# Delta stage with a pair's heads on the two partition halves, x turned on the host

## The chip, the cores and the metric

One core of a Trainium2 chip. The metric is the device time of one execution in microseconds, from start to end, the median of several runs. Lower is better.

## What is computed

One layer of a streaming encoder, for 4096 new frames of one stream and 16 frames of each of 8 running streams (the "sample" rows). Cut to what matters here:

```python
xn = rms_norm(h, ln_g)                       # x * rsqrt(mean(x^2)) * ln_g
proj = xn @ w_in                             # columns: q/k/v of group A, a, b, z_a, then group B
# group A, 8 heads of 64: causal conv (4 taps) + SiLU, l2-normed q and k, decay g, beta
# per block of 64 frames, S the 64x64 state of a head:
v_new = u - w @ S                            # u, w from a triangular solve within the block
o     = q_dec @ S + qk @ v_new
S     = S * g_tot + k_tail.T @ v_new
o_a   = rms_norm(o, gdn_norm_g) * silu(z_a)
# group B, 8 heads: softmax attention over a band of 576 keys, times silu(z_b)
h = h + concat(o_a, o_b) @ w_out
h = h + sigmoid(h @ w_gate) * rms_norm(p @ w_ple, ple_norm_g)
```

## The kernel before, in words

All arithmetic is float32; the large products are made of three passes over a high and a low part (`matmul3`, lines 86 to 90). The stages run one after the other with a barrier of all engines between them: `project_a` (q/k/v of group A, the convolution, the gates), `project_b` (the other columns, and the triangular systems), `delta` (the recurrence), the sample stages, `attend`, `combine`. Every engine has its own queue, written out by hand in program order, and semaphores between the queues; SP issues all DMAs.

**Stage A** (`project_a`) works on blocks of two tiles of 128 frames, twelve groups of 128 output columns each. While block b is multiplied, the two tiles of b+1 are prepared: `load_x` (L276), `square` on ScalarE (L442), `norm` on GpSimd (rstd, L393 to L395), `scale` on ScalarE (x times rstd, in place, L446), eight 128x128 `transposes` on TensorE into PSUM (L560), `full` on VectorE (times ln_g, L662), `split_hi` on ScalarE (L453), `split_lo` on VectorE (L668). `spill` stores the turned, normed x (`xT`) for `project_b`. The transposes stand behind groups 3 and 8. TensorE waits for `lo_ok` ahead of each block. VectorE convolves each group (L682, L685) after ScalarE copies it out of PSUM (L513). The weights are split at the start, in 32 pieces through seven buffers: `hi_part` on ScalarE (L458), `lo_part` on VectorE or GpSimd in turn (L265); 16 pieces before block 0, 16 within it.

**Delta stage** (`delta`): 32 tiles of two chunks of 64 frames; n is the chunk, t the tile. A pair p holds heads 2p and 2p+1 (e = 0, 1); the state `S` has a pair's heads on partitions 0 to 63 and 64 to 127. Everything with frames on the partitions (values `vt`, residuals `r`, new values `vn`, keys `kt`, outputs `o`) has chunk 0 of the tile on partitions 0 to 63 and chunk 1 on 64 to 127, all heads side by side. `half_heads(x)` are the four heads of pairs 2x and 2x+1. For one chunk:

- TensorE: `keys_state` (L1738), `queries_state` (L1749), `solved` (L1757), `outputs` of the chunk before (L1765), `new_state` (L1774), each for x = 0 and 1, four matmuls of 64x64x64 at a time. In an even chunk `prepare` follows: four whole transposes of the next tile's keys into `psA` (L1721), four of its values into `psB` (L1723).
- VectorE: `residual` (L1829, one operation per head), after odd chunks `keys` of the next tile (L1813), `state` (L1841, one operation per two pairs), in even chunks `out_sums` of the tile before (L1847).
- ScalarE: `decayed` (L1693), `new_values` (L1673), `out_rows` of the chunk before (L1680), `out_square` in even chunks (L1686), `values` of the next tile in odd ones (L1664).
- GpSimd, once a tile: `gate` (L1631), `scaled` (the next tile's queries, L1624), `out_norm` of the tile before (L1635 to L1646).
- SP, once a tile: store of the output rows (L1578), two loads of the query row scales (L1569), `UQ` (the solved systems, L1571), the gate rows (L1574), every second tile `conv_T` (L1559). It runs six tiles ahead.

Ahead of the loop the per-frame scales are loaded as rows and turned by 32 small transposes (L1781).

Of the kernel before, what the change touches and what calls it, by code (L numbers as in the profile page):

```python
# [31 lines left out]
P = 128  # L32
# [82 lines left out]
def project_a(nc, d, s):  # L115
# [13 lines left out]
    RING, SLOTS = 6, 7  # L129
# [4 lines left out]
    with ExitStack() as stack:  # L134
# [3 lines left out]
        x_raw = [ph.sb(f"a_x{i}", [P, D]) for i in range(2)]  # L138
        squares = ph.sb("a_squares", [P, D], mybir.dt.bfloat16)
        x_full = [ph.sb(f"a_x_full{i}", [P, KT, P]) for i in range(2)]  # L140
# [30 lines left out]
        psT = ph.ps("a_psT", [P, KT * P])  # L171
# [16 lines left out]
        x_in = [ph.sem(f"a_x_in{i}") for i in range(2)]  # L188
# [3 lines left out]
        scaled = ph.sem("a_scaled")  # L192
        xT_ps = ph.sem("a_xT_ps")
# [19 lines left out]
        spilled = [ph.sem(f"a_spilled{i}") for i in range(2)]  # L213
# [48 lines left out]
        def lo_part(eng, m, done):  # L262
            k, a, b = PIECES[m]
            eng.wait_ge(w_hi_ok, m + 1)
            eng.tensor_tensor(w_lo[:, k, a:b], stage[m % SLOTS][:, 0:b - a], w_hi[:, k, a:b].bitcast(F32),  # L265
                              ALU.subtract).then_inc(done, 1)
# [4 lines left out]
        def _(sp):  # L271
            def load_x(t):
                if t >= 2:
                    sp.wait_ge(xT_ps, t - 1)
                src = d.x_p[order[t] * P:(order[t] + 1) * P, :] if t != SAMPLE else d.x_s
                sp.dma_start(x_raw[t % 2][:, :], src).then_inc(x_in[t % 2], 16)  # L276

            def spill(t):
                sp.wait_ge(full_ok, t + 1)
                sp.dma_start(d.xT[order[t]], x_full[t % 2][:, :, :]).then_inc(spilled[t % 2], 16)  # L280
# [36 lines left out]
            load_x(0)  # L317
            with nc.allow_non_contiguous_dma(reason="small per-channel constants, once"):
                sp.dma_start(lnT[:, :], d.ln_g.rearrange("(k p) -> p k", p=P)).then_inc(ln_in, 16)
            load_x(1)  # L320
            for m, (k, a, b) in enumerate(PIECES):
# [5 lines left out]
                if m == 5:  # L327
                    with nc.allow_non_contiguous_dma(reason="small per-channel constants, once"):
# [4 lines left out]
                        sp.dma_start(alog[0:HA, :], d.a_log.rearrange("(h o) -> h o", o=1)).then_inc(consts, 16)  # L333
                if m == 16:
                    load_x(2)
                    spill(0)
                if m == 20:
                    load_x(3)
                    spill(1)
            for b in range(BLOCKS):  # L340
# [5 lines left out]
                for x, t in enumerate(tiles_of(b + 1)):  # L346
                    if t + 2 < TILES:
                        load_x(t + 2)
# [19 lines left out]
            for i in range(2):  # L368
                sp.wait_ge(stored[i], 16 * (BLOCKS // 2))
                sp.wait_ge(kq_out[i], 32 * 2 * BLOCKS)  # L370
                sp.wait_ge(spilled[i], 16 * ((TILES + 1 - i) // 2))
# [7 lines left out]
        def _(pool):  # L379
# [36 lines left out]

            norm(0)
            norm(1)
            for i in range(HALVES // 2):
                lo_part(pool, 2 * i + 1, w_lo_g)  # L420
            for b in range(BLOCKS):
# [15 lines left out]
        def _(e):  # L437
            def square(t):
                e.wait_ge(x_in[t % 2], 16 * (t // 2 + 1))
# [3313 lines left out]
```

## Time and profile before

| | us |
|---|---|
| median of three runs | 3620.63 (3614.67 to 3621.94) |
| profiled execution, its own time | 3616.96 |
| its span | 3615.2 |
| TensorE busy | 3311.5 (92%) |
| VectorE busy | 2440.0 (67%) |
| ScalarE busy | 1519.8 (42%) |
| GpSimd busy | 1348.5 (37%) |
| mean granted TensorE clock | 0.965 |
| stage A, first to last main matmul | 26.2 to 751.0 |
| delta stage, first to last state matmul | 1739.9 to 2051.9 |

PE is TensorE's matmuls, PEld its weight loads (a float32 matmul shows as two passes, each with a load), DVE VectorE, ACT ScalarE, POOL GpSimd, SP the engine that issues DMAs. Matmuls overlap, so a busy TensorE can still be waiting for the next step; the starts of weight loads show its pace better. Idle time stands before an instruction, with what ended it.

### The profile page before, as it was taken

The numbers are of one execution on the slowest core, as the hardware profiler recorded it, in microseconds if no ns is written. First come the engines' busy times: TensorE is split into PE (matmuls) and PEld (weight loads), VectorE is DVE, ScalarE is ACT, GpSimd is POOL, SyncE is SP. The second block draws the span as 40 slices with busy tenths as digits, with TensorE's granted clock in tenths as the row PEclk, the third lists the DMA queues.
The fourth block names the chain that finished last, engine by engine and source line by source line (L and its number), as shares of the span: only waits on it lengthen the run. The fifth ranks groups of instructions, "written<-read, shape, count | busy, mean of one in ns | idle before, by whom it ended". The sixth has DMA issues, their size and how long they took to land. (4 is left out here: it accounts for less than half of the span.)

```text
span 3615.2 us, 68943 instructions
## 1 busy us (share of the span) xinstructions
PE 3311.5 (92%) x26156; PEld 2827.1 (78%) x26156; DVE 2440.0 (67%) x4770; ACT 1519.8 (42%) x2959; POOL 1348.5 (37%) x1561
## 2 busy tenths in 40 slices
PE   7999999969998999999777667999997999999998
PEld 6999899957886888888676544888885788778887
DVE  7777687745997878682465454766666655666765
ACT  5555455533223323211455423666664222344443
POOL 3222222219896836310466610000001233455664
PEclk9999999989999999999799878999998999999999
DMA  5343244344436552523866355222223544322221
GB/s 157 109 112 113 86 118 114 100 146 132 135 104 184 173 152 103 147 79 113 254 212 228 81 146 187 89 74 75 88 74 129 186 155 148 112 76 100 79 105 63
DMA packets 330646, 455.19 MB, mean 126 GB/s; under 512 B 189555, under 2 KB 212371, under 8 KB 325702
## 3 DMA queue, kind: packets, MB, share of 16 engines
q1 hardware_dynamic: 330318, 450.77, 39.5%
q8 instruction: 211, 3.46, 0.4%
q14 instruction: 117, 0.96, 0.1%
HBM read 276.56 MB, written 176.76 MB: 125 GB/s over the span
## 5 line engine op out<-in xcount | busy, mean ns | idle before, releaser
L88 PE MATMUL b_psP<-b_w_hi,b_xT_hi 128*128 128x512 f32 x1320 | 519.2, 393 | 41.2 <-DVE b_xT_lo L1319 24.3
L89 PE MATMUL b_psP<-b_w_lo,b_xT_hi 128*128 128x512 f32 x1320 | 517.1, 392 | 0.0
L90 PE MATMUL b_psP<-b_w_hi,b_xT_lo 128*128 128x512 f32 x1320 | 516.6, 391 | 0.0
L88 PE MATMUL a_psG<-a_xT_hi,a_w_hi 128*128 128x256 f32 (+1 forms) x1536 | 454.0, 296 | 21.1 <-DVE a_xT_lo L668 19.5
L89 PE MATMUL a_psG<-a_xT_lo,a_w_hi 128*128 128x256 f32 (+1 forms) x1536 | 441.5, 287 | 0.0
L90 PE MATMUL a_psG<-a_xT_hi,a_w_lo 128*128 128x256 f32 (+1 forms) x1536 | 441.0, 287 | 0.0
L88 PE MATMUL h_psM<-h_w_hi,h_c_hi 128*128 128x512 f32 x928 | 371.1, 400 | 37.8 <-DVE h_w_lo L3257 16.3
L89 PE MATMUL h_psM<-h_w_lo,h_c_hi 128*128 128x512 f32 x928 | 366.3, 395 | 0.0
L90 PE MATMUL h_psM<-h_w_hi,h_c_lo 128*128 128x512 f32 x928 | 366.1, 394 | 0.0
L3241 POOL TENSOR_TENSOR h_c_lo<-h_c_lo_whole,h_c_hi 128x512 fp32r<-128x512 f32 x162 | 219.2, 1380 | 325.0 <-ACT h_c_hi L3342 325.0
L88 PEld LDWEIGHTS a_psG<-a_xT_hi,a_w_hi 128*128 128x128 f32 x1536 | 295.3, 192 | 42.7 <-DVE a_xT_lo L668 23.5
L88 PEld LDWEIGHTS b_psP<-b_w_hi,b_xT_hi 128*128 128x128 f32 x1320 | 249.8, 189 | 99.7 <-DVE b_xT_lo L1319 48.0
L685 DVE SCALAR_TENSOR_TENSOR a_act<-a_raw,a_taps,a_act 128x256 f32<-128x256 f32 x576 | 289.1, 502 | 20.6
L89 PEld LDWEIGHTS a_psG<-a_xT_lo,a_w_hi 128*128 128x128 f32 x1536 | 295.7, 192 | 0.0
L90 PEld LDWEIGHTS a_psG<-a_xT_hi,a_w_lo 128*128 128x128 f32 x1536 | 295.5, 192 | 0.0
L90 PEld LDWEIGHTS b_psP<-b_w_hi,b_xT_lo 128*128 128x128 f32 x1320 | 249.7, 189 | 52.4
L3540 DVE TENSOR_TENSOR h_acc<-h_acc,h_psM 128x512 f32<-128x512 f32 x322 | 210.0, 682 | 119.7 <-PE h_psM L90 119.6
L89 PEld LDWEIGHTS b_psP<-b_w_lo,b_xT_hi 128*128 128x128 f32 x1320 | 250.1, 189 | 51.4
L408 POOL COPY a_halo<-a_raw 128x3 f32<-128x3 f32 x192 | 74.3, 387 | 503.3 <-ACT a_raw L513 501.9
L2652 DVE CUSTOM_DVE_ANT_0 f_neg<-f_score,f_bias 128x640 f32<-128x640 f32 (+4 forms) x256 | 192.4, 780 | 82.4 <-PE f_score L2552 52.7
L88 PEld LDWEIGHTS h_psM<-h_w_hi,h_c_hi 128*128 128x128 f32 x928 | 177.3, 191 | 80.0 <-issue 33.4
L1282 ACT ACTIVATE b_rows<-b_psP 128x512 f32<-128x512 f32 x99 | 59.3, 599 | 390.6 <-PE b_psP L90 383.4
(378 smaller groups left out, 7375.1 us busy)
## 6 DMA issues: line engine op xcount, KB each, us to landing
rows_b<-b_rows SPq DMA_DIRECT2D x165, 256.0 KB, 2.2
b_x_full<-xT SPq DMA_DIRECT2D x78, 512.0 KB, 4.3
qkvB<-a_act SPq DMA_DIRECT2D x16, 1536.0 KB, 5.4
d_conv_T<-qkvB SPq DMA_DIRECT2D x16, 1536.0 KB, 10.8
xT<-a_x_full SPq DMA_DIRECT2D x33, 512.0 KB, 3.3
out<-h_rows SPq DMA_DIRECT2D x33, 512.0 KB, 2.7
a_x<-in_x_prompt SPq DMA_DIRECT2D x32, 512.0 KB, 4.4
kq<-a_kq SPq DMA_DIRECT2D x128, 128.0 KB, 2.8
```

The lines of the kernel that those rows point to most:

```text
L88: nc.tensor.matmul(out, x_hi, w_hi, start=first, stop=False)
L89: nc.tensor.matmul(out, x_hi, w_lo, start=False, stop=False)
L90: return nc.tensor.matmul(out, x_lo, w_hi, start=False, stop=last)
L408: pool.tensor_copy(halo[:, g, :], x[:, N:]).then_inc(halo_ok, 1)
L685: v.scalar_tensor_tensor(out, x[:, j:j + N], taps[:, j, g:g + 1], out, ALU.mult, ALU.add).then_inc(conv, 1)
L1282: e.activation(rows[u % ROWS][:, :], psP[u % BANKS][:, :], ACT.Copy if seg == V else ACT.Silu).then_inc(taken, 1)
L2652: v.tensor_tensor_reduce(neg[h % 2][:, 0:n], score[h % 2][:, 0:n], bias[:, h, KEYS - n:], -1.0 / ROOT, BIG, ALU.add, ALU.min, low[a.b][:, ...
L3241: eng.tensor_tensor(c_lo[i][:, :, :], c_raw[i][:, :, :], c_hi[i][:, :, :].bitcast(F32), ALU.subtract)\
L3540: v.tensor_tensor(there, there, psM[u % BANKS][:, :], op).then_inc(folded, 1)
```

## The change

In the delta stage the axis of frames within a chunk (64) lies on the partitions twice, once for the even and once for the odd head of each pair. Outputs of head e go to partitions of half e, in PSUM too, where a pair's two halves now share a bank (`psC` is two banks instead of four, `psO` is one per chunk). Keys and values are still turned by whole transposes, in four steps of two, and the copies out of PSUM (four a tile for each) move the odd heads across. Values are copied two chunks ahead, keys one. The sum of squares for the norm moves from the even to the odd chunk. Loads and stores of frames' rows are split in two by head parity; to keep them contiguous the columns of z_a and the rows of w_out come reordered from the host. The small transposes of the start become 64.

In stage A the host gives x also turned. ln_g goes into the weights, where they are split; the turned x is multiplied by a row of rstd that one transpose spreads over the partitions; it has three buffers (`XBUFS`). `project_b` multiplies its weights by ln_g too.

```diff
@@ project_a
+            def load_xT(t):
+                if t >= XBUFS:
+                    sp.wait_ge(spilled[t % XBUFS], 16 * (t // XBUFS))
+                    sp.wait_ge(lo_ok, t - XBUFS + 1)
+                    sp.wait_ge(ab_ok, t - XBUFS + 1)
+                src = d.xT_p[order[t] * P:(order[t] + 1) * P, :] if t != SAMPLE else d.xT_s
+                sp.dma_start(x_full[t % XBUFS][:, :, :], src.rearrange("p (k n) -> p k n", k=KT)).then_inc(xT_in[t % XBUFS], 16)
...
-            def scale(t):
-                e.wait_ge(rstd_ok, t + 1)
-                e.activation(x_raw[t % 2][:, :], x_raw[t % 2][:, :], ACT.Copy, scale=rstd[:, t % 2:t % 2 + 1]).then_inc(scaled, 1)
...
             def hi_part(m):
-                e.activation(w_hi[:, k, a:b], stage[m % SLOTS][:, 0:b - a], ACT.Copy).then_inc(w_hi_ok, 1)
+                x = stage[m % SLOTS][:, 0:b - a]
+                if m % 2:
+                    e.activation(x, x, ACT.Copy, scale=lnT[:, k:k + 1]).then_inc(w_scaled, 1)
+                    e.wait_ge(w_scaled, m // 2 + 1)
+                    e.activation(w_hi[:, k, a:b], x, ACT.Copy).then_inc(w_hi_ok, 1)
+                else:
+                    e.activation(w_hi[:, k, a:b], x, ACT.Copy, scale=lnT[:, k:k + 1]).then_inc(w_hi_ok, 1)
...
-                for k in range(KT):
-                    last = nc.tensor.transpose(psT[:, k * P:(k + 1) * P], x_raw[t % 2][:, k * P:(k + 1) * P], ident[:, :])
-                last.then_inc(xT_ps, 1)
+                nc.tensor.transpose(psB[:, 0:P], rstd[:, a:a + 1].to_broadcast([P, P]), ident[:, :]).then_inc(rstd_ps, 1)
...
+                v.tensor_tensor(x[:, :, :], x[:, :, :], psB[:, 0:P].unsqueeze(1).to_broadcast([P, KT, P]), ALU.mult)\
+                    .then_inc(full_ok, 1)
@@ delta
-        psC = [ph.ps(f"d_psC{i}", [P, 2, W]) for i in range(2)]
-        psO = ph.ps("d_psO", [P, 2, W])[:, :, 0:PAIRS * C].rearrange("p e (a c) -> p e a c", a=PAIRS)
+        psC = [ph.ps(f"d_psC{i}", [P, W]) for i in range(2)]
+        psS, psV, psD = ([x[:, m * 2 * C:(m + 1) * 2 * C].rearrange("p (a c) -> p a c", a=2) for x in psC] for m in range(3))
+        psO = [ph.ps(f"d_psO{i}", [P, W])[:, 0:HALF].rearrange("p (a c) -> p a c", a=PAIRS) for i in range(2)]
...
-                    last = nc.tensor.matmul(psS[x][c, e, p - 2 * x, :], raw(t)[rows_e, PAIRS + p, c], old[rows_e, p, :],
+                    last = nc.tensor.matmul(psS[x][rows_e, a, :], raw(t)[rows_e, PAIRS + p, cols], old[rows_e, p, :],
...
-                    last = nc.tensor.matmul(psV[x][c, to], UQ[t % BUFS][c, e * PAIRS + p, 0, :], r[c, at], start=True, stop=True)
+                    last = nc.tensor.matmul(psV[x][rows_e, a, :], UQ[t % BUFS][rows_e, c, p, 0, :], r[c][rows_e, p, :], start=True, stop=True)
...
             for n in range(NCH):
+                ahead = n // 2 + 1
                 keys_state(n, 0)
                 keys_state(n, 1)
                 queries_state(n, 0)
+                queries_state(n, 1)
+                if ahead < NT:
+                    (turn_values, turn_keys)[n % 2](ahead, n % 2)
                 solved(n, 0)
-                queries_state(n, 1)
                 solved(n, 1)
+                if ahead < NT and n % 2 == 0:
+                    turn_values(ahead, 1)
                 if n:
                     outputs(n - 1, 0)
+                    outputs(n - 1, 1)
                 new_state(n, 0)
-                if n:
-                    outputs(n - 1, 1)
                 new_state(n, 1)
-                if n % 2 == 0 and n // 2 + 1 < NT:
-                    prepare(n // 2 + 1)
+                if ahead < NT and n % 2 == 0:
+                    turn_keys(ahead, 0)
...
                     for a in range(2):
-                        for e in range(2):
...
+                        p = 2 * x + a
+                        op = v.scalar_tensor_tensor(r[c][:, p, :], psS[x][:, a, :], key_gain[:, n, p:p + 1], vt[t % 2][:, c, p, :],
+                                                    ALU.mult, ALU.add)
...
-                if n % 2 == 1 and t + 1 < NT:
-                    keys(t + 1)
+                if n + 1 < NCH:
+                    keys(n + 1)
                 state(n)
-                if n % 2 == 0 and t:
+                if n % 2 == 1 and t:
                     out_sums(t - 1)
@@ delta_sample
-            sp.dma_start(d.mixed[at, 0:W], out[:, :]).then_inc(stored, 16)
+            for e in range(2):
+                sp.dma_start(d.mixed[at, e * W // 2:(e + 1) * W // 2].rearrange("r (a c) -> r a c", c=C),
+                             out[:, :].rearrange("r (a e c) -> r a e c", e=2, c=C)[:, :, e, :]).then_inc(stored, 16)
```

## Rows read from the trace of the kernel before

**Rows 1.** Stretches of the run: us, busy us and count by engine, PEclk, DMA share, GB/s

```profile
448.00:752.00 304.00, 301.45 (x2849) 284.26 (x2848) 236.19 (x466) 164.38 (x307) 73.24 (x200) 1.00 0.35 101
1740.00:2054.00 314.00, 251.45 (x5347) 228.42 (x5350) 186.81 (x702) 181.28 (x509) 204.96 (x187) 0.96 0.64 204
```

**Rows 2.** Timeline of VectorE over one tile of the delta stage: start, us

```profile
1882.47 0.29 DVE L1841 TENSOR_TENSOR d_S<-d_sgt,d_psC 128x128 f32<-128x128 f32 x1 [1.15 <-PE d_psC L1774]
...
1884.13 0.69 DVE L1847 TENSOR_REDUCE d_oss<-d_osq 128x8 f32<-128x512 f32 x1 [0.83 <-ACT d_osq L1686]
1884.85 1.72 DVE L1829 SCALAR_TENSOR_TENSOR d_r<-d_psC,d_key_gain,d_vt 64x64 f32<-64x64 f32 x8
...
1887.72 0.29 DVE L1841 TENSOR_TENSOR d_S<-d_sgt,d_psC 128x128 f32<-128x128 f32 x1 [0.43 <-PE d_psC L1774]
...
1889.26 1.62 DVE L1829 SCALAR_TENSOR_TENSOR d_r<-d_psC,d_key_gain,d_vt 64x64 f32<-64x64 f32 x8 [0.70 <-ACT d_vt L1664]
1892.02 0.29 DVE L1841 TENSOR_TENSOR d_S<-d_sgt,d_psC 128x128 f32<-128x128 f32 x1 [1.15 <-PE d_psC L1774]
```

**Rows 3.** Timeline of TensorE's weight loads over the same tile

```profile
1882.53 0.14 PEld L1765 LDWEIGHTS d_psO<-d_vn,d_UQ 64*64 64x64 f32 x1
1882.57 0.26 PEld L1774 LDWEIGHTS d_psC<-d_vn,d_kt 64*64 64x64 f32 x6
1882.90 0.42 PEld L1721 LDWEIGHTS d_psA<-d_ident,d_conv_T 128*128 128x128 f32 x4
...
1883.92 0.55 PEld L1738 LDWEIGHTS d_psC<-d_S,d_conv_T 64*64 64x64 f32 x16 [0.16 <-issue]
...
1888.06 0.31 PEld L1738 LDWEIGHTS d_psC<-d_S,d_conv_T 64*64 64x64 f32 x8
...
1890.16 0.54 PEld L1757 LDWEIGHTS d_psC<-d_r,d_UQ 64*64 64x64 f32 x8 [1.01 <-DVE d_r L1829]
...
1891.50 0.19 PEld L1774 LDWEIGHTS d_psC<-d_vn,d_kt 64*64 64x64 f32 x3
```

**Rows 4.** ScalarE's copies out of PSUM: a group by shape, and one line's durations

```profile
L1673 ACT ACTIVATE d_vn<-d_psC 64x256 f32<-64x256 f32 x96 | 36.3, 378 | 76.1 <-PE d_psC L1757 76.1
...
L509 ACT ACTIVATE a_raw_s<-a_psG x12: 277/278/280, 392.7 to 447.2; 128x128 f32<-128x128 f32 x12
```

**Rows 5.** Timeline of GpSimd over the same tile, first and last of six

```profile
1884.90 0.20 POOL L1635 TENSOR_TENSOR d_ovar<-d_oss,d_floor 128x8 f32<-128x8 f32 x1 [2.72 <-DVE d_oss L1847]
...
1890.46 1.26 POOL L1624 TENSOR_TENSOR d_Qd<-d_conv_T,d_sc 128x512 f32<-128x512 f32 x1
```

**Rows 6.** DMA from 1780 to 1990 (share of 16 engines, us to landing), and SP's waits

```profile
DMA packets 17382, 46.65 MB, mean 222 GB/s; under 512 B 1931, under 2 KB 7484, under 8 KB 15932
...
q1 hardware_dynamic: 17340, 46.06, 67.8%
...
mixed<-d_out SPq DMA_DIRECT2D x22, 256.0 KB, 6.3
...
SPq L1569 <- PE d_psO L1765: 162.8, 26, 7.6
```

**Rows 7.** Timeline in stage A: TensorE's loads, ScalarE, VectorE; last the start's weights

```profile
248.92 0.19 PEld L88 LDWEIGHTS a_psG<-a_xT_hi,a_w_hi 128*128 128x128 f32 x1 [0.79 <-DVE a_xT_lo L668]
...
281.24 0.90 PEld L560 LDWEIGHTS a_psT<-a_ident,a_x 128*128 128x128 f32 x8
...
292.83 0.19 PEld L88 LDWEIGHTS a_psG<-a_xT_hi,a_w_hi 128*128 128x128 f32 x1 [0.78 <-DVE a_xT_lo L668]
...
276.41 1.14 ACT L446 ACTIVATE a_x<-a_x,a_rstd 128x1024 f32<-128x1024 f32 x1
...
279.57 0.35 DVE L682 TENSOR_SCALAR a_act<-a_raw,a_taps 128x256 f32<-128x256 f32 x1 [1.70 <-ACT a_raw L513]
...
291.56 1.22 DVE L668 TENSOR_TENSOR a_xT_lo<-a_x_full,a_xT_hi 128x1024 fp32r<-128x1024 f32 x1
...
22.24 2.98 ACT L458 ACTIVATE a_w_hi<-a_act 128x384 fp32r<-128x384 f32 x7
```

More of the change, by code:

```diff
@@ L525, in _ @@
                             square(ahead[0])
-                        if g == 1:
-                            scale(ahead[0])
                         if g == 4:
@@ L532, in _ @@
                             square(ahead[1])
-                        if g == 6:
-                            scale(ahead[1])
                         if g == 9:
@@ L539, in _ @@
                             square(ahead[2])
-                        if g == 9:
-                            scale(ahead[2])
                         if g == 11:
@@ L1121, in _ @@
             load_x(0)
+            with nc.allow_non_contiguous_dma(reason="small per-channel constants, once"):
+                sp.dma_start(lnT[:, :], d.ln_g.rearrange("(k p) -> p k", p=P)).then_inc(ln_in, 16)
             for k in range(KT):
@@ L1586, in _ @@
+            for e in range(2):
+                sp.dma_start(rows[PAIRS:2 * PAIRS, :, e, :], d.ssqT[e * PAIRS:(e + 1) * PAIRS, :]
+                             .rearrange("a (n i) -> a n i", i=C)).then_inc(rows_in, 16)
             for t in range(BUFS):
@@ L1696, in _ @@
             values(0)
+            values(1)
             for n in range(NCH):
@@ L1766, in outputs @@
                 last.then_inc(t_o, 1)
             def new_state(n, x):
-                t, c, old = places(n)
+                t, c, cols, old = places(n)
                 pe.wait_ge(s_vn, 2 * n + x + 1)
-                if x == 0 and n % 2 == 0:
-                    pe.wait_ge(v_kt, t + 1)
-                for p, e, h, at, rows_e in half_heads(x):
-                    last = nc.tensor.matmul(psD[x][rows_e, p - 2 * x, :], kt[t % 2][c, at], vn[c, at], start=True, stop=True)
+                if x == 0:
+                    pe.wait_ge(v_kt, 2 * (n + 1))
@@ L1775, in new_state @@
+                for p, a, rows_e in half_heads(x):
+                    last = nc.tensor.matmul(psD[x][rows_e, a, :], kt[t % 2][rows_e, c, p, :], vn[c][rows_e, p, :], start=True, stop=True)
                 last.then_inc(t_ds, 1)
-            pe.wait_ge(rows_in, 16 * (1 + NCH // 8))
-            for t in range(NT):
-                to = (psA, psB)[t // (NT // 2)]
-                at = t % (NT // 2) * 3 * H
-                last = nc.tensor.transpose(to[:, at:at + 3 * H], rows[:, t * P:(t + 1) * P], ident[0:3 * H, 0:3 * H])
+            pe.wait_ge(rows_in, 16 * 10)
@@ L1782, in _ @@
+            for n in range(NCH):
+                to = (psA, psB)[n // NT]
+                at = n % NT * 3 * PAIRS
+                last = nc.tensor.transpose(to[:, at:at + 3 * PAIRS], rows[:, n, :, :].rearrange("k e i -> k (e i)"),
+                                           ident[0:3 * PAIRS, 0:3 * PAIRS])
             last.then_inc(t_rows, 1)
             pe.wait_ge(v_scal, 2)
-            prepare(0)
+            for c in range(2):
+                turn_values(0, c)
+            for c in range(2):
+                turn_keys(0, c)
@@ L1840, in state @@
                         v.wait_ge(t_qs, 2 * (n - 1) + x + 1)
-                    v.tensor_tensor(new[:, two, :], sgt[:, two, :], psD[x][:, :, :], ALU.add).then_inc(v_state, 1)
+                    v.tensor_tensor(new[:, two, :], sgt[:, two, :], psD[x], ALU.add).then_inc(v_state, 1)
             def out_sums(t):
@@ L3709, in laid_out @@
     out = {}
+    pairs, half = s.HA // 2, s.HA * s.DV
+    first = s.QKV + 2 * s.HA
+    za = np.reshape(inputs["w_in"][0][:, first:first + half], (s.D, pairs, 2, s.DV))
+    out["w_za"] = np.ascontiguousarray(np.transpose(za, (0, 2, 1, 3)).reshape(s.D, half))
+    mix = np.reshape(inputs["w_out"][0][0:half], (pairs, 2, s.DV, s.D))
+    out["w_out_a"] = np.ascontiguousarray(np.transpose(mix, (1, 0, 2, 3)).reshape(half, s.D))
+    out["xT_p"] = columns_first(inputs["x_prompt"][0])
+    out["xT_s"] = columns_first(np.reshape(inputs["x_sample"], (s.DECB * s.DECT, s.D)))
     out["pT_p"] = columns_first(inputs["p_prompt"][0, 0])
```

330 lines of the change are left out of this document (180 added, 150 removed).

## The prediction

> **What bounds the kernel now.** I read the granted clock and the busy time by stretch, then the waits of the delta stage, then its timeline engine by engine, then the ends of the blocks in the first projection. The stages run one after the other with barriers between, so each is costed alone.
>
> In the first projection (stage A) TensorE is busy for 301 of 304 us, in the delta stage for 251 of 314 at a granted clock of 0.96 [rows 1]; no other engine is full in either. The delta stage is a ring of short steps from engine to engine; the residuals of one chunk in two wait in it 0.70 for ScalarE's copy of the values [rows 2]. The timeline gives the period. A new state of an even chunk starts at 1882.47, of the odd one at 1887.72, of the next even one at 1892.02: 5.25 and 4.30, 9.55 us for a tile of two chunks [rows 2]. 32 tiles make 306 us.
>
> VectorE shows where they go [rows 2]. In the long chunk it sits until 1884.13 for the sum of squares, which waits for ScalarE, and the residuals start 2.38 after the state; in the short one they start 1.54 after it, held by the copy of the values. Each chunk has eight residual operations on 64 partitions, 1.62 to 1.72 in all, 0.2 apiece.
>
> TensorE's weight loads show the cost of a group of four 64x64 matmuls (two passes each, eight loads) [rows 3]. Where two heads lie on different row halves, as for the keys against the state, 8 loads take 0.31; less one load's 0.14 and plus a step of 0.06, 0.23 a group. Where all four lie on one quarter of the array, as for the solving matmuls, 8 take 0.54, so 0.46 a group. Eight whole transposes hold the line from 1882.90 to 1883.92, and the last small load before them began about 1882.69: 1.17 for eight, 0.87 of it streaming at 0.11 apiece, so some 0.3 goes into the turn to the full array and back.
>
> **The change, delta stage.** A pair's two heads go to the two diagonal quarters. All ten groups of a chunk then cost 0.23 (solving and output groups before: 0.46), if both quarters work at once as now. Residuals fall from eight to four operations on 128 partitions, 0.8 us less before the second half's solve. The values are copied two chunks ahead and the sum of squares moves a chunk later, so both waits of VectorE go. What is late next is TensorE's own order. I write it from the start of a state. Keys against state at 0.34 (1887.72 to 1888.06 [rows 2, 3]), the second half, behind two state operations of 0.29, at 0.59, queries 0.82 to 1.28, two transposes (0.22 plus 0.3) to 1.79, solve to 2.26, in an even chunk two more transposes to 2.77, outputs of the chunk before to 3.23, then the new state, whose first load precedes the state's start by 0.52 (1891.50 to 1892.02). Even chunk: 3.75. An odd chunk follows two key transposes, so its keys start at 0.45; solve 1.89 to 2.35, outputs to 2.81, state at 3.33. The tile takes 7.1.
>
> Cover. Residuals start at 0.9, or 1.25 behind the moved sum, and two suffice for the first solve at 1.6 to 1.7, before 1.79. ScalarE's copy of new values goes from 0.38 (64x256) to 0.28, the 128x128 row [rows 4]. Its 181 us [rows 1] are 5.7 a tile; four such copies give back 0.4, the two output copies, half as long a row each, another 0.4, and four half copies of the values at 0.38 in place of one whole of some 0.6 add 0.9: 5.8 of 7.4, hidden by its idle time. The key product becomes four half-partition products on VectorE, hidden in its idle time. GpSimd does a tile in 6.8 us (1884.90 to 1891.72 [rows 5]), and it now starts later: its sums land 1.25 into the next tile, its scaled queries for the tile after at 8.1, wanted at one tile plus 0.82. That asks for 7.3; shared between the two rings, 7.2.
>
> DMA. SP issues 8.5 transfers a tile instead of 5.5. It runs six tiles ahead and stood 162.8 us waiting for outputs to free a buffer [rows 6], 5 a tile, which covers three more issues. The engines are 67.8% taken [rows 6], 6.5 us a tile. The change halves the pieces of UQ, of the gate rows and of the output store: 384 more pieces a tile to the present 790 (17382 in 22 tiles). If time goes by bytes it stays 6.5; if by pieces, 9.6. I take 7, near the bytes, since most of the present time already belongs to megabyte transfers, and put 0.2 on the tile for queueing: **7.4**.
>
> Sum: 32 x (9.55 - 7.4) = -69. The start has 64 small transposes for 32, at 0.11: +3.5. At the end two output norms stand behind the last state instead of one and a part: +2. Delta: **-63**.
>
> **Stage A.** The eight transposes of x per tile and ScalarE's scaling of x (1.14 us) go; one transpose of the scale comes. TensorE's eight transposes take 0.90; less one of 0.14 it gets back about 0.76 a tile. But a block (two tiles, 248.92 to 292.83, so 43.9 us) does not end with TensorE: the next block's first matmul waits 0.78 for the low part of x from VectorE [rows 7]. VectorE runs without a gap from 279.57 to 292.78, from the convolution of group 7 on, and that one waited 1.70 for ScalarE's copy of the group, which the queue has behind the scaling (276.41) and the gates' logarithm. Without the scaling that copy is 1.14 earlier, up to 1.9 if the earlier transposes' 0.76 comes through too; TensorE alone allows 2.1. I take 1.5 for each of 15 blocks: -22. VectorE's product by the scale replaces the one by ln_g at the same size; the loads of turned x have a third buffer and a block of time; SP does them where it did x. Start: eight of the first sixteen weight pieces take a second pass on ScalarE (seven take 2.98, so 0.43 each [rows 7]) and half a megabyte more goes ahead of them: between 0 and +8, I take +2. Stage A: **-20** (-8 to -31).
>
> **The rest.** The second projection folds ln_g into its weights: same operations, but its first waits for a load of single floats: 0 to +4, taken +1. The sample stage splits its gate load and output store into 256-byte pieces; the store's end is waited for. A store of that tile lands after 6.3 now [rows 6]; half as much again is +3, nothing is 0; +1.5. The last stage reads as many bytes as before.
>
> Together -20 + 1 - 63 + 1.5 = -80.5. The profiled execution took 3616.96 (span 3615.2), the median of three is 3.7 above: **3536** for the profiled run, **3540** for the median.
>
> **A rule against this.** In [rows 3] the heads of one group write to two PSUM banks; the change puts both row halves' outputs in one bank, on different partitions. No row shows that. The Trainium skill (TensorEngine Tiling (Array Packing), Restrictions and Gotchas) says that different row tiles cannot access the same PSUM bank simultaneously. By that rule the groups would fall back to one after the other, the rival below. The same page (Tiling Modes) has it that a change of tiling mode drains the array; the 0.3 around the transposes agrees, and the change makes four such turns a tile instead of one, which is in the sum.
>
> **Rivals.**
> (a) *The two halves exclude each other* (slower). Every group then costs the 0.46 of the one-quarter row. Even chunk: keys and queries 0.34 to 2.19, transposes to 2.70, solve 3.62, 4.13, outputs 5.06, state 0.75 later, 5.8; odd 5.65. The tile takes 11.45, 32 x 1.9 = +61; with +5.5, -20 and +2.5: **3666** profiled, 3670 median. For: nothing in the kernel now runs so. Against: the partitions written are disjoint. It decides from a tile of about 9.9 us on, where the delta stage gives back what stage A brings.
> (b) *Transfers bound the delta stage.* Pieces, not bytes, set the time: 8.5 to 9.6 a tile, at 9 -18 + 5.5; total **3587** profiled. Against: a six-tile lead and 32% idle. For: the 49% more pieces.
> (c) *Stage A is held elsewhere*: VectorE's order, not ScalarE's scaling, sets the blocks; -5 instead of -20: **3551**.
> (d) *The ring is tighter than I write it*: turns to the full array overlap with waits, tile 6.9: **3520**.
>
> **Chances.** Forecast 0.56, (a) 0.07, (b) 0.13, (c) 0.12, (d) 0.12. Range of the median 3512 to 3588: (d) with a block gain of 2.1 at the low end, (b) at the high; (a) and the worst of (b) stay out. A measurement of this kernel can tell 0.2%, 7 us, from no change. Faster 0.91, same 0.02, slower 0.07: only (a) and the far end of (b) are not faster.
>
> **What would show it.** Right: new states 7.1 to 7.6 apart per tile, the solving group's 8 loads in 0.31, no wait of the residuals for the values, residuals 0.4 a half; blocks of stage A 42.4 apart. Wrong: 8 loads of the key group in 0.54 (a); waits of the scaled queries or transposes for DMA in mid-stage (b); blocks still 43.9 apart (c); a first matmul later than 30 us would take the start's term away. A state that waits for ScalarE would mean that its idle 1.6 us a tile do not lie where I need them.

## The result, and the profile after

| | before | after |
|---|---|---|
| median of four runs, us | 3620.93 (3614.67 to 3621.94) | 3579.84 (3579.68 to 3580.40) |
| ratio, 95% interval | | 0.9893 (0.9881 to 0.9905) |
| profiled execution, span | 3616.96, 3615.2 | 3579.74, 3577.9 |
| end of stage A's products | 751.0 | 732.0 |
| delta stage, start to its end | 1721.7 to 2062.6, 340.9 | 1701.5 to 2020.0, 318.5 |
| new states, first to last | 309.0 | 273.4 |

The forecast was 3540; the change brought 41 us instead of 81. Stage by stage, ends against ends in the two traces: stage A -19.1 (forecast -20), second projection -1.1 (+1), delta stage -22.4 (-63), sample stages -0.5 (+1.5), attention +4.4 and last stage +0.5 (0); the delta stage ends here with its last output row, and the stores behind it take 0.9 longer. That makes the -37.3 of the spans. So the miss is one stage, and inside it there are two: its ring is disturbed, and its start is long.

The two stretches of [rows 1] in the kernel after, moved to where their stages now lie, and under them the first 82 us of the attention in the kernel after:

```profile
448.00:728.00 280.00, 278.54 (x2619) 262.19 (x2618) 225.84 (x444) 144.30 (x279) 70.11 (x189) 1.00 0.43 126
1720.00:2034.00 314.00, 245.28 (x5436) 205.21 (x5435) 161.07 (x548) 187.48 (x608) 218.77 (x198) 0.91 0.83 215
...
2176.00:2258.00 82.00, 68.89 (x535) 50.88 (x537) 44.02 (x119) 37.55 (x106) 1.72 (x5) 0.80 0.40 130
```

The third stretch in the kernel before:

```profile
2218.00:2300.00 82.00, 68.05 (x585) 51.26 (x587) 47.13 (x125) 40.08 (x111) 1.79 (x6) 0.88 0.42 136
```

Stage A is as full of TensorE as before. In the delta stage the DMA share rose from 0.64 to 0.83 and the granted clock fell from 0.96 to 0.91, which means that TensorE now stands still for longer. The attention's first 82 us got a granted clock of 0.88 before and 0.80 now; nothing was changed there, and in the same 82 us TensorE began 535 matmuls instead of 585. It is not the change that does this: from its first instruction to the last stage's first, the attention takes 548.4 to 549.4 us in nine of the traces of this case and 551.8 to 553.9 in the other six, and kernels of both kinds are in both groups (run 3, on the old kernel, 553.3 with a clock of 0.80; run 1, on the new one, 548.4 with 0.88). Which one an execution gets is some 4 us of chance.

VectorE in an undisturbed tile of the delta stage after the change, the counterpart of [rows 2]:

```profile
1950.77 0.68 DVE L1898 TENSOR_REDUCE d_oss<-d_osq 128x8 f32<-128x512 f32 x1
1951.37 0.85 DVE L1880 SCALAR_TENSOR_TENSOR d_r<-d_psC,d_key_gain,d_vt 128x64 f32<-128x64 f32 x4
1952.25 0.88 DVE L1868 TENSOR_TENSOR d_kt<-d_psA,d_scal 64x256 f32<-64x256 f32 x2
1954.07 0.52 DVE L1892 TENSOR_TENSOR d_S<-d_sgt,d_psC 128x128 f32<-128x128 f32 x2 [0.94 <-PE d_psC L1817]
1955.05 0.86 DVE L1880 SCALAR_TENSOR_TENSOR d_r<-d_psC,d_key_gain,d_vt 128x64 f32<-128x64 f32 x4 [0.46 <-PE d_psC L1781]
1956.11 0.87 DVE L1868 TENSOR_TENSOR d_kt<-d_psA,d_scal 64x256 f32<-64x256 f32 x2 [0.20 <-PE d_psA L1756]
1957.43 0.52 DVE L1892 TENSOR_TENSOR d_S<-d_sgt,d_psC 128x128 f32<-128x128 f32 x2 [0.46 <-PE d_psC L1817]
```

The residuals take 0.86 instead of 1.72 and wait for no copy of values; the two half states stand together in one row. From 1954.07 to 1957.43 is 3.36; the other kind of chunk takes 3.73 wherever nothing disturbs it. Together 7.09 a tile, where I had worked out 3.33, 3.75 and 7.1. TensorE's weight loads in the same tile, the counterpart of [rows 3]:

```profile
1950.91 0.31 PEld L1781 LDWEIGHTS d_psC<-d_S,d_conv_T 64*64 64x64 f32 x8
...
1955.01 0.55 PEld L1792 LDWEIGHTS d_psO<-d_S,d_Qd 64*64 64x64 f32 x16
1955.63 0.20 PEld L1756 LDWEIGHTS d_psA<-d_ident,d_conv_T 128*128 128x128 f32 x2
1956.00 0.54 PEld L1799 LDWEIGHTS d_psC<-d_r,d_UQ 64*64 64x64 f32 x16 [0.17 <-DVE d_r L1880]
1956.46 0.55 PEld L1807 LDWEIGHTS d_psO<-d_vn,d_UQ 64*64 64x64 f32 x16
1956.93 0.55 PEld L1817 LDWEIGHTS d_psC<-d_vn,d_kt 64*64 64x64 f32 x16
```

The first row is the first key group of the chunk before, alone: 8 loads in 0.31. A row of 16 loads is two groups, and takes 0.54 where one group of the solving matmuls took that alone. The two heads of a pair do work at once, although both write to one PSUM bank: rival (a) is out.

So the ring is what I forecast, and 63 steps from state to state of it make 223.2 us (32 of 3.36, 31 of 3.73). The trace has 273.4. The 50.2 us between them I call the **excess**. Here is where it lies, TensorE's weight loads in two places:

```profile
1768.68 0.31 PEld L1807 LDWEIGHTS d_psO<-d_vn,d_UQ 64*64 64x64 f32 x8 [0.17 <-ACT d_vn L1712]
1773.32 0.54 PEld L1807 LDWEIGHTS d_psO<-d_vn,d_UQ 64*64 64x64 f32 x8 [4.33 <-issue]
...
1890.31 0.14 PEld L1817 LDWEIGHTS d_psC<-d_vn,d_kt 64*64 64x64 f32 x1
1893.40 0.54 PEld L1817 LDWEIGHTS d_psC<-d_vn,d_kt 64*64 64x64 f32 x15 [2.96 <-issue]
```

TensorE stops in the middle of a row of matmuls, after the 8th load of 16 or after the first. No semaphore stands there and the profile names no releaser ("issue"). Counted from the stage's first weight load, the pauses over 0.5 us lie behind loads 248, 372, 620, 993, 1117, 1242, 1367, 1615, 1987, 2112, 2733, 2981, 3355, 3479, 3604 and so on: 20 of 22 within three loads of a multiple of 124.26, and those 20 sum to 34.8 us. I call such a place a **border**. With 124.26 loads go as many matmuls and, by the count between 1780 and 1960 (3568 loads, 3570 matmuls, 214 waits for semaphores), 7.5 waits: from border to border there are 256 of TensorE's instructions. So the pauses are tied to a place in TensorE's program, not to data. A chunk behind a long pause is longer too, since the clock has fallen:

```profile
1883.30:1887.10 3.80, 2.05 (x56) 1.69 (x52) 1.40 (x7) 0.51 (x2) 1.00 1.01 363
1887.10:1893.90 6.80, 2.25 (x54) 1.75 (x50) 1.37 (x7) 0.51 (x2) 1.00 0.88 197
1893.90:1898.80 4.90, 2.64 (x55) 2.16 (x49) 1.53 (x7) 0.51 (x2) 0.65 0.99 257
1898.80:1902.60 3.80, 2.06 (x52) 1.64 (x48) 1.44 (x7) 0.51 (x2) 1.00 0.91 375
```

These are four chunks on end, with the busy time on the tile psC alone; the last three columns are clock, DMA share and GB/s. The second holds the 2.96 pause (+3.07). The third has no pause, but after that standstill a granted clock of 0.65, so most of it was at the lower of the two levels (1.2 GHz, 0.5), and it is 1.4 too long; at 1.00, 2.4 GHz, the fourth is whole again. The DMA queues over most of the stage, to stand against [rows 6], and what SP waits for there:

```profile
DMA packets 29526, 50.96 MB, mean 243 GB/s; under 512 B 3274, under 2 KB 21948, under 8 KB 27942
q1 hardware_dynamic: 29478, 50.29, 85.7%
q8 instruction: 34, 0.56, 1.2%
d_conv_T<-qkvB SPq DMA_DIRECT2D x12, 1536.0 KB, 9.3
mixed<-d_out SPq DMA_DIRECT2D x52, 128.0 KB, 4.8
...
SPq L1594 <- PE d_psO L1807: 49.7, 23, 5.1
```

The share rose from 67.8% to 85.7%. Instructions come by DMA too, in packets of 16 KB (0.56 MB in 34); between 1745 and 2010 there are 42 of them, one for 246 weight loads and matmuls of TensorE, close to the 248.5 from border to border. Data is hardly waited for after the start: SP still stands 49.7 us waiting for TensorE to free buffers.

The start. The first new state comes 35.2 us into the stage; before the change it came after 22.8. TensorE and SP in the kernel after:

```profile
1719.40 3.56 PE L1824 MATMUL d_psA<-d_ident,d_rows 12*128 12x12 f32 x32 [22.02 <-DMA d_rows<-ssqT]
1722.81 3.56 PE L1824 MATMUL d_psB<-d_ident,d_rows 12*128 12x12 f32 x32
1729.61 1.09 PE L1756 MATMUL d_psB<-d_ident,d_conv_T 128*128 128x128 f32 x4 [3.25 <-DMA d_UQ<-UQ]
...
1706.41 2.08 SPq L1618 DMA_DIRECT2D d_rows<-krow  x2
1708.54 2.44 SPq L1621 DMA_DIRECT2D d_rows<-ssqT  x2
```

The row factors land 17.9 us into the stage; the 64 small transposes take 7.0; and the first tile is then not there yet.

### The profile page after: what moved, and what is told of

The parts are those of the page before. It is cut to its first block and busy times, and to the rows that moved or that the text cites. A ratio compares the mean times of both kernels' runs of the same rounds, so it can differ in the third digit from the quotient of the medians.

```text
span 3577.9 us, 68709 instructions
## 1 busy us (share of the span) xinstructions
PE 3280.1 (92%) x25957; PEld 2777.6 (78%) x25957; DVE 2408.6 (67%) x4610; ACT 1506.8 (42%) x3038; POOL 1349.7 (38%) x1562
## 5 line engine op out<-in xcount | busy, mean ns | idle before, releaser
L701 DVE SCALAR_TENSOR_TENSOR a_act<-a_raw,a_taps,a_act 128x256 f32<-128x256 f32 x576 | 307.5, 534 | 20.6
```

The lines of the kernel that those rows point to most:

```text
L701: v.scalar_tensor_tensor(out, x[:, j:j + N], taps[:, j, g:g + 1], out, ALU.mult, ALU.add).then_inc(conv, 1)
```

## The experiments

Five theories of the excess. **P**, from my rival (b): smaller pieces fill the DMA engines. **B**: the same bytes on a shorter tile do, whatever their pieces. **E**: TensorE pauses by itself, without transfers. After the first four runs, two that say how transfers do it: **F**, TensorE's next block of instructions comes late through busy DMA engines, and **D**, data comes late, and the pauses follow from that. An excess is read from one execution of each kernel. In run 1, with nearly the time of the changed kernel, it is 56.3 instead of 50.2, so a difference of some 6 us between two of them says little.

**1. UQ in 4 KB pieces again.**

```diff
-    d.UQ = scratch("UQ", [2, s.DV, NT, s.HA, 2, s.DV])
+    d.UQ = scratch("UQ", [s.DV, NT, s.HA, 2, 2, s.DV])
```

> The same computation; in the scratch matrix UQ the two chunks of a tile lie side by side, so the delta stage fetches it in 4 KB pieces instead of 2 KB, as before the change. Theory P (the size of the pieces fills the DMA engines: 8.2 us of a tile's 8.7 are DMA time, against 6.65 with the old pieces): 64 pieces fewer a tile, 0.8 to 1.0 us of DMA time less, tile 8.7 to some 7.9, 3550 to 3562 us. Theory B (the bytes moved on a shorter tile, whatever their pieces): no change, 3576 to 3583 us. Theory E (TensorE's pauses come from the engine itself, not from transfers): no change either.

3582.26 (3577.97 to 3584.56), ratio 0.9900 (0.9886 to 0.9914): no change, P misses by 20 us.

**2. All pieces as before.**

```diff
-                for e in range(2):
-                    there = za[z][e * C:(e + 1) * C, :].rearrange("i (c w) -> i c w", c=2)
-                    sp.dma_start(there, tokens(d.rows_b, t, e)).then_inc(za_in[z], 16)
+                sp.dma_start(za[z][:, :], d.rows_b[t * P:(t + 1) * P, 0:W]).then_inc(za_in[z], 16)
...
+                sp.dma_start(d.mixed[t * P:(t + 1) * P, 0:W], out[t % 2][:, :]).then_inc(stored[t % 2], 16)
```

> As uq4k, and the gates za and the outputs mixed are moved in whole 2 KB rows by one DMA each, as before the change (the gates' and outputs' chunks then lie in the wrong places: time only). The bytes are the same. Theory P: the DMA time of a tile is back at 6.6 to 6.8 us, tile 7.3 to 7.6, delta stage 38 to 45 us shorter, 3535 to 3545 us, and TensorE's pauses inside its groups (33 us in all) fall under 8 us. Theory B: 6.7 us of DMA time on a 7.1 us ring still collide, tile 8.4 to 8.7, 3570 to 3582 us. Theory E: 3576 to 3583 us.

3590.14 (3583.77 to 3600.50), ratio 0.9929 (0.9914 to 0.9944): 10 us slower than the changed kernel and past what any of the three theories forecast. The gates' and outputs' chunks lie in the wrong places here, for the time alone. The excess is 60.2, the pauses at the borders 42.5. P is refuted; why whole rows make it worse stays open.

**3. The other way round: the old kernel with the new pieces.** UQ, gates and outputs go by two DMAs each, of halves of a row.

```diff
-                sp.dma_start(UQ[b][:, :, :, :], d.UQ[:, :, t].rearrange("e j h x i -> (e j) h x i")).then_inc(ok, 16)
+                for e in range(2):
+                    sp.dma_start(UQ[b][:, e * PAIRS:(e + 1) * PAIRS, :, :], d.UQ[:, :, t, e * PAIRS:(e + 1) * PAIRS].rearrange("e j h x i -> (e j) h x i")).then_inc(ok, 16)
```

> The kernel before, with the pieces of the change: UQ by two DMAs of 2 KB pieces, gates and outputs by two DMAs of 1 KB pieces. Theory P: DMA time of a tile goes from 6.65 to some 8 us, but its tile has 9.55; a few more pauses of TensorE, 0 to +12 us on 3621. Theory B and theory E: 0, within 3 us. If the number of DMAs that SP issues were the cause rather than the pieces, SP's waits would vanish here and tiles grow past 9.8.

3617.53, ratio to the kernel before 0.9999 (0.9989 to 1.0008). The whole delta stage in one row, first of the kernel before, then of this one (after PE, PEld, DVE, ACT and POOL come clock, DMA share, GB/s):

```profile
1755.00:2040.00 285.00, 227.19 (x4960) 206.25 (x4958) 171.69 (x643) 168.22 (x471) 191.14 (x174) 0.99 0.64 205
```

```profile
1755.00:2040.00 285.00, 228.43 (x4985) 207.60 (x4987) 174.17 (x653) 169.10 (x473) 193.17 (x177) 0.99 0.65 206
```

Half again as many pieces cost 0.01 of DMA share. Pieces of 1 and 2 KB are as good as 2 and 4 KB here, by bytes.

**4. Without most of the loads.**

```diff
-                if t + BUFS < NT:
-                    load(t + BUFS)
-            eng.wait_ge(c_in[t % BUFS], 16 * LOADS * (t // BUFS + 1))
+            eng.wait_ge(c_in[t % BUFS], 16 * LOADS)
```

> UQ, its row factors and the gates are loaded for the first tiles only, and these stand in for all later ones (time only): of the delta stage's transfers only the convolved tiles and the outputs are left. Theories P and B: pauses inside TensorE's groups under 3 us in all, every chunk at 3.36 and 3.73 after the start, tile 7.1, delta stage some 50 us shorter: 3525 to 3535 us. Theory E: the pauses stay, 3570 to 3580 us.

3550.58 (3549.55 to 3553.61), ratio 0.9815 (0.9803 to 0.9828): 29 us of the changed kernel go. The excess falls to 19.9 us, 14 of it before 1780, where the first tiles' loads still run (DMA share 0.95 from 1740 to 1780, 0.47 from 1800 to 1940). E is out. UQ, its row factors and the gates of later tiles are left out, so the outputs are not those of the layer. I had expected 3525 to 3535; the start, as long as in the changed kernel, and this remainder are the difference.

**5. The loads back, but nobody reads them.** This tells F from D.

```diff
+                b = t if t < 2 else 2 + t % 4
...
-            eng.wait_ge(c_in[t % BUFS], 16 * LOADS * (t // BUFS + 1))
+            eng.wait_ge(c_in[t % 2], 16 * LOADS)
```

> As few_loads (the first tiles' UQ, factors and gates stand in for all later ones; time only), but every later load is still issued, with the same pieces and waits of SP, into buffers that nobody reads. So the traffic is that of the changed kernel and no engine waits for it. Theory F (TensorE's pauses stand 124.3 weight loads apart because its next 16 KB of instructions come late through full DMA engines): the pauses return at those places, 25 us or more in all, 3572 to 3582 us. Theory D (the time goes with data that comes late, and the pauses follow from that): as few_loads, 3548 to 3555 us.

3579.84, ratio 0.9899 (0.9880 to 0.9917): the changed kernel's time to the microsecond. The excess is 50.5, with 29.8 in 15 pauses at the borders. Load 2981 of the stage, the same as in the changed kernel at 1890.31 (and in run 1, where it cost 3.37), first in this kernel, then in run 4, whose 16 loads go through without a stop:

```profile
1895.11 0.14 PEld L1824 LDWEIGHTS d_psC<-d_vn,d_kt 64*64 64x64 f32 x1
1899.30 0.40 PEld L1824 LDWEIGHTS d_psC<-d_vn,d_kt 64*64 64x64 f32 x6 [4.05 <-issue]
```

```profile
1876.66 0.55 PEld L1819 LDWEIGHTS d_psC<-d_vn,d_kt 64*64 64x64 f32 x16
```

Traffic alone, which no engine waits for, brings the whole loss back, at the same places of the program. That is F.

The records of the 16 KB packets show the wait itself. In the changed kernel, TensorE crosses a border at 1885.0. The queue of these packets has none between 1885.1 and 1890.8, and between 1890.8 and 1892.2 one:

```profile
q8 instruction: 1, 0.02, 5.6%
```

It begins at 1890.88 and has landed at 1892.12; the pause that began behind the load of 1890.31 ends at 1893.40, 1.28 later. All 20 pauses at borders end 1.3 to 1.8 us after such a packet has landed. In none of the 13 kernels whose delta stage is told of here (before, changed, runs 1 to 10 and 13) does a block of 256 instructions begin less than 1.2 us after the landing. Between 1760 and 1975 each packet begins 0.6 to 6.8 us after TensorE has begun the block before, and it lands 4.7 after that (median of 34). A block lasts 5.2, so what lands more than about 3.8 after that makes TensorE stand: 25 of the 34 do, 18 of them by enough for a pause over 0.5 us. The packet's own transfer is 1.2 of that (0.95 in the kernel before); the rest goes by before it begins.

**6. The 1.5 MB load in two halves, a tile apart.**

```diff
-                sp.dma_start(conv_T[x % 3][:, :, :], d.qkvB[x]).then_inc(conv_in[x % 3], 16)
+                for i in (0, 1) if part is None else (part,):
+                    six = slice(6 * i, 6 * i + 6)
+                    sp.dma_start(conv_T[x % 3][:, six, :], d.qkvB[x][:, six, :]).then_inc(conv_in[x % 3], 16)
```

> The same computation; the convolved tiles' load of 1.5 MB for each two tiles (12 KB pieces) is cut into two of 6 KB pieces, issued one tile apart. Theory F with the burst as the cause of a late fetch (pauses came 5 to 10 us after each such load was issued): pauses fall by half, 3560 to 3570 us. Theory F with the mean load of the engines as the cause: 3577 to 3583 us. Theory D: no change.

3577.10 (3573.96 to 3579.76), ratio 0.9884 (0.9868 to 0.9901). The excess is 40.1, the pauses at the borders 23.8 instead of 34.8, a third less and not half. They are of the fastest of the four executions (3573.96); the median is only 3 us below the changed kernel's, as the mean load would have it and 7 above what bursts would. Bursts are at most a part of it.

**7. A shorter prefetch.**

```diff
-    BUFS, ZBUFS = 6, 8
+    BUFS, ZBUFS = 4, 6
```

> The same computation; the delta stage prefetches 4 tiles ahead instead of 6 (gates 6 instead of 8), so that less is queued in the first 60 us, where the DMA share was 1.0 and the longest pauses stood. Theory F: pauses of the first 80 us (14 us) fall by half, later ones stay, -5 to -12 us: 3568 to 3575 us. Theory D: shallower prefetch makes data later: 3582 to 3600 us.

3577.69 (3572.29 to 3582.71), ratio 0.9886 (0.9868 to 0.9904); excess 42.2. The time can't tell it from the changed kernel and is 3 above the 3568 to 3575 that I expected; its excess is 8 us less, with 26.3 at the borders, and four tiles ahead are enough for the data.

**8. The row factors' loads from ScalarE's queue.**

```diff
-                        sp.dma_start(rows[first:first + PAIRS, x::2, e, :],
+                        e.dma_start(rows[first:first + PAIRS, x::2, h, :],
```

> The same computation; the ten loads of the row factors at the start of the delta stage (256 B pieces, landed 18 us into the stage, 9 us in the kernel before) are issued by ScalarE, beside SP's loads of the first tiles instead of ahead of them. If SP's queue order costs the start: first new state 5 to 9 us earlier, 3571 to 3576 us. If the row loads themselves take their 17 us wherever they are issued, and the first tile was ready behind them anyway: 0 to -4 us.

3601.84 (3594.91 to 3603.42), ratio 0.9951 (0.9936 to 0.9965), 22 us slower, a miss of both. TensorE waited for them until 61.2 us into the stage:

```profile
PE d_psA L1824 <- DMA d_rows<-ssqT: 61.2, 1, 61.2
```

Issued beside megabytes, the 256-byte pieces did not get through between them. They belong ahead of all else, or must be fewer. The first six tiles' data lay ready long before in this run, and still the excess was 38.3.

**9. Together, and the row factors as whole rows.** Runs 6 and 7, and the factors come with a chunk on each partition, in 2 KB pieces, and are turned by 24 matmuls.

```diff
+            for k, src in ((0, d.ketr), (2, d.krow)):
+                sp.dma_start(rows[:, k, :, :, :].rearrange("n e a i -> n (e a i)"), src.rearrange("n h i -> n (h i)")).then_inc(rows_in, 16)
...
+                    last = nc.tensor.matmul(to[e * C:(e + 1) * C, at:at + NCH], rows[:, k // PAIRS, e, k % PAIRS, :], ident[0:NCH, 0:NCH], start=True, stop=True)
```

> The same computation, three edits of the changed kernel together: the convolved tiles' load in two halves and the shallower prefetch (as run before, apart), and the row factors of the delta stage loaded as whole 2 KB rows, one chunk on each partition, by four DMAs, and turned by 24 small matmuls instead of 64 transposes. Theory F: excess of the chunks 50 to some 33 us; and the start, if the 256 B pieces and the 64 transposes make it long (rows landed 18 us into the stage, 7.1 us of transposes): first new state 24 to 27 us into the stage instead of 35. Together 25 us: 3552 to 3562 us. If the start is the time of the first tile's own transfers behind whatever stands ahead of them: first state still past 32 us, 3566 to 3574 us.

3563.75 (3553.97 to 3564.62), ratio 0.9840 (0.9822 to 0.9857): faster than both kernels, 16 us below the changed one and 2 above my range.

```profile
1711.13 1.55 PE L1826 MATMUL d_psA<-d_ident,d_rows 64*64 64x64 f32 x24 [11.16 <-DMA d_rows<-ssqC]
1712.44 1.52 PE L1826 MATMUL d_psB<-d_ident,d_rows 64*64 64x64 f32 x24
1719.14 1.09 PE L1757 MATMUL d_psB<-d_ident,d_conv_T 128*128 128x128 f32 x4 [5.18 <-DMA d_UQ<-UQ]
```

The stage starts at 1704.1. The rows land after 7.0 us instead of 17.9, are turned in 2.8 instead of 7.0, and the first state comes after 22.4 instead of 35.2: all of the start's loss is back. The excess is 44.5 and not the 33 that I expected; runs 6 and 7 had 40.1 and 42.2, so nothing shows that those two edits add up.

**10. One load in eight less.** The queries' row factors come for the first six tiles only.

```diff
-                for e in range(2):
+                for e in range(2) if t < BUFS else ():
```

> The delta stage's row factors of the queries (0.25 MB of a tile's 2.05) are loaded for the first six tiles only and stand in later (time only). Theory F with the mean load of the DMA engines as the cause: DMA time a tile 12% less, pauses of TensorE fall by a third or more, 3562 to 3571 us. With the 1.5 MB bursts alone as the cause: 3576 to 3582 us.

3562.53 (3560.45 to 3567.02), ratio 0.9844 (0.9828 to 0.9860): 17 us for 0.25 of 2.05 MB a tile. Excess 31.5, pauses at borders 18.6. The traffic counts, and steeply. These loads are 12% of the bytes and 256 of a tile's 1174 pieces, 22%; this run can't tell the two apart, but fewer pieces for the same bytes brought no gain in runs 1 and 2; the DMA share does not order the runs (0.89 here, 0.86 in run 2 with more than twice the pauses).

**11 and 12. Stage A, one half of the change taken back at a time.** First ScalarE:

```diff
+                        if g == 1:
+                            repeat(ahead[0])
...
+                e.activation(squares[:, :], squares[:, :], ACT.Copy).then_inc(again, 1)
```

> The changed kernel with one more copy of ScalarE over 1024 columns for each tile of stage A, at the places where the scaling of x stood before the change. If a block of stage A is set by ScalarE's order of copies, as I argued: blocks from 42.1 back to 43.2 to 43.9, +17 to +27 us: 3597 to 3607 us. If TensorE's transposes set it: within 2 us of 3580.

3592.37 (3587.74 to 3601.85), ratio 0.9929 (0.9912 to 0.9947): 5 us below the range for ScalarE and 10 above that for TensorE. Then TensorE:

```diff
-                nc.tensor.transpose(psB[:, 0:P], rstd[:, a:a + 1].to_broadcast([P, P]), ident[:, :]).then_inc(rstd_ps, 1)
+                for k in range(8):
+                    last = nc.tensor.transpose(psB[:, 0:P], rstd[:, a:a + 1].to_broadcast([P, P]), ident[:, :])
+                last.then_inc(rstd_ps, 1)
```

> The changed kernel with the one transpose a tile of stage A made eight times, as many as stood there before, with ScalarE as the change has it. If TensorE's transposes set the block: 42.1 to 43.5 or more, +20 us. If ScalarE's order did: TensorE has 0.3 to 0.6 a block to spare, blocks 42.1 to 42.8, 0 to +10 us: 3580 to 3590 us.

3597.03 (3588.01 to 3605.61), ratio 0.9936 (0.9920 to 0.9953), 7 us past my range. The first weight loads of two blocks on end, in the changed kernel, with ScalarE's copy, with eight transposes:

```profile
247.96 0.19 PEld L88 LDWEIGHTS a_psG<-a_xT_hi,a_w_hi 128*128 128x128 f32 x1 [0.50 <-DVE a_xT_lo L684]
290.05 0.19 PEld L88 LDWEIGHTS a_psG<-a_xT_hi,a_w_hi 128*128 128x128 f32 x1 [0.50 <-DVE a_xT_lo L684]
```

```profile
253.57 0.19 PEld L88 LDWEIGHTS a_psG<-a_xT_hi,a_w_hi 128*128 128x128 f32 x1 [1.48 <-DVE a_xT_lo L697]
296.64 0.19 PEld L88 LDWEIGHTS a_psG<-a_xT_hi,a_w_hi 128*128 128x128 f32 x1 [1.48 <-DVE a_xT_lo L697]
```

```profile
251.41 0.19 PEld L88 LDWEIGHTS a_psG<-a_xT_hi,a_w_hi 128*128 128x128 f32 x1 [0.20 <-issue]
294.71 0.19 PEld L88 LDWEIGHTS a_psG<-a_xT_hi,a_w_hi 128*128 128x128 f32 x1 [0.20 <-issue]
```

Blocks of 42.09, 43.07 and 43.30 us, against 43.91 before [rows 7]. ScalarE's scaling alone gives back 0.98 of 1.82, the transposes alone 1.21. With the transposes TensorE is full: 14 of them at 0.11 are 1.5, less the 0.3 by which the wait could shrink.

**13. Are busy DMA engines enough?** The kernel before, with a load that nobody reads.

```diff
+                    sp.dma_start(spare[:, :, :], d.qkvB[t // 2 % 16]).then_inc(spare_in, 16)
```

> The kernel before, with one more load of 1.5 MB for each two tiles of the delta stage into a buffer that nobody reads, issued by SP beside the others: DMA share from 0.65 to some 0.87, the changed kernel's, on its own slower ring (a block of 16 KB of TensorE's instructions lasts 7.1 us there, 5.25 in the changed kernel). If full DMA engines alone make instructions late: pauses 124 weight loads apart, 10 us or more in all, +10 to +30 us: 3630 to 3650 us. If it takes the faster ring too: fewer than three such pauses, within 4 us of 3618.

3621.78, ratio to the kernel before 1.0009 (0.9993 to 1.0025): no loss. Behind the first two tiles its chunks take 5.25 and 4.30 as in [rows 2], but for two that are 1.1 and 0.8 longer and a few by under 0.6; the kernel before has four such chunks, 0.5 to 1.25 longer.

```profile
1755.00:2040.00 285.00, 228.09 (x4945) 206.90 (x4947) 171.86 (x647) 167.99 (x471) 191.07 (x174) 0.99 0.83 287
```

The share is 0.83, where the changed kernel has 0.93 between 1745 and 1960 and run 10 has 0.89, and 287 GB/s are more than any of those moved. So a high load alone does not do it. The packets of instructions are as late here as in the changed kernel: between 1760 and 1975 they land 4.5 us (median) after TensorE has begun the block before, against 4.7 there. But on the old ring TensorE takes 9.55 x 124.26 / 168 loads a tile = 7.1 us to use up a block of instructions; on the new one 7.09 x 124.26 / 168 = 5.2 us. What lands within about 5.7 us costs nothing on the old ring. TensorE still pauses at four borders here, for 3.0 us in all, and at three in the kernel before, for 3.3; these too end 1.3 to 1.5 us after a landing. What run 13 leaves open is a load as high as the changed kernel's 0.93.

## Why the prediction was wrong

- **The ring** was right to 0.01 a tile: 3.36 and 3.73 against 3.33 and 3.75, residuals 0.43 a half, no wait for the values. The 7.2 for GpSimd's loop was not seen; undisturbed tiles run at 7.09.
- **The bank.** Sixteen loads of two groups take 0.54 with both halves in one bank. The rule of the Trainium skill that I weighed (TensorEngine Tiling (Array Packing), Restrictions and Gotchas: different row tiles can't access the same bank simultaneously) does not hold for these matmuls, which write to different partitions of the bank; the measurement (8 loads in 0.31, 16 in 0.54) decides.
- **DMA is the step that failed:** "I take 7, near the bytes [...] and put 0.2 on the tile for queueing: 7.4." Pieces cost nothing (run 3), which I had right. But the queueing was sized as a delay of data that six tiles of lead would cover; the excess was 50.2 us, 1.6 a tile where the sum had 0.2. It hit the one stream that has no lead of six tiles, TensorE's own instructions. Run 5 shows that the traffic does it without any data being waited for; run 4 that it goes with the traffic; run 13 that the old, slower ring hardly feels it. That it is the fetch of instructions rests on the places, 256 instructions apart, and on the packets' records: all 20 pauses end 1.3 to 1.8 us after a packet of instructions has landed. The part of the excess that is not in these pauses, 15.4 us, goes in part with the lower clock behind them (1.4 behind the one of 2.96); the rest I did not take apart.
- **Rival (b)** came near the time (3587 against 3579.74) by a mechanism that runs 1 to 3 refute. The measured median lies inside my range only for its sake, which is luck; and the range was drawn too narrow at that end, since (b)'s 3587 is 3591 in the median (the other end should have been 3515, not 3512). Its tile of 8.5 to 9.6 was met on average (7.09 + 1.6 = 8.7), for another reason.
- **The delta stage's start**, "64 small transposes for 32, at 0.11: +3.5", was +12.4. The transposes cost 3.4 as I had them; I left out the loads of the row factors: ten instead of nine, 512 more pieces of 256 bytes since ssqT's whole rows are cut, and each onto 4 partitions instead of 8; they land 9.1 later (17.9 against 8.8). I had counted DMAs for the tiles only. Which of pieces and partitions it is was not separated; run 9 takes both away and the rows land after 7.0. The tail was +0.9 for +2.
- **Stage A** was right in sum by two errors: undisturbed blocks gained 1.82 and the 15 together 24.2, 1.6 each, instead of 1.5, since neither ScalarE nor TensorE alone held them (runs 11 and 12), and block 1 starts 5.4 later instead of 2.
- **The rest:** the sample stages did not feel their small pieces (-0.5 for +1.5). The attention's +4.4 came with a lower granted clock in its first 82 us; it is the chance of the one profiled execution, seen with the old kernel too, and no term of the change. Why the clock comes out at 0.80 or 0.88 there stays open.

In sum: -85.8 for the ring (223.2 against 309.0), +50.2 excess, +12.4 start, +0.9 tail make -22.3 for the delta stage.

## What to carry to other kernels

Where a change makes a ring of small matmuls faster beside heavy transfers, TensorE's instructions are a stream of their own: look for pauses without a releaser in the middle of a group, count the weight loads between them, lay them beside the landings of the instruction packets, and see whether bytes can be taken out of the stage; a deep prefetch helps data, not instructions. At the start of a stage, count the pieces of each load ahead of the first use: row factors in 256-byte pieces landed 9 us late here, and 11 us earlier as whole rows. Two costs that share a block may both be needed to hold it, so take each back alone before naming one.

## What the runs showed of the hardware

- Two float32 64x64 matmuls on the two diagonal quarters of the array run at once into one PSUM bank, on disjoint partitions: 16 weight loads in 0.54 us, the time of 8 on one quarter.
- TensorE pauses at fixed places, 256 of its instructions apart (here 124.26 weight loads and as many matmuls), for up to 4.3 us, when the DMA engines are busy and it goes through such a block in 5.2 us. Each pause ends 1.3 to 1.8 us after a 16 KB packet of instructions has landed. In the changed kernel these landed 4.7 us (median) after TensorE had begun the block before. The pauses sum to 34.8 us in the changed kernel (DMA share 0.93, 249 GB/s), to 42.5 in run 2 (0.86, 237), to 18.6 in run 10 (0.89, 241) and to 10.2 in run 4 (0.55, 156 from 1745 to 1940), there mostly at the start; at 7.1 us a block they sum to 3.0 us, even at 0.83 and 287 GB/s.
- After the pause of 2.96 us the next chunk got a granted clock of 0.65 and took 1.4 us more.
- Bytes in pieces of 1 and 2 KB kept the DMA engines as busy as in 2 and 4 KB (0.65 against 0.64).
- Loads of 256-byte pieces that are issued from a second queue beside megabyte loads landed 61 us into the stage, with all of those.
